# Four mixers and two feed-forwards in one kernel: 83 steps of two stage lists stand ahead of another one

## What is computed

```python
def layer0(h):
    h = sandwich(h, pre, post, even_mixer_2)      # stage "diff"
    return sandwich(h, pre, post, swiglu)         # stage "ffn0"
def layer1(h):
    h = sandwich(h, pre, post, odd_mixer_2)       # stage "ssm"
    return sandwich(h, pre, post, swiglu)         # stage "ffn1"
```

```python
def even_mixer_2(t):
    proj = t @ w_in
    y_a = diff_attention(proj[..., :1536])   # 4 heads: softmax(q1 k1) - lam * softmax(q2 k2), times v, rmsnorm
    y_b = conformer_conv(proj[..., 1536:])   # u * sigmoid(g), depthwise causal conv of 31 taps, layernorm, silu
    return concat([y_a, y_b]) @ w_out
def odd_mixer_2(t):
    proj = t @ w_in
    y_c = s5_ssm(proj[..., :256])            # complex diagonal state space, 16 groups of 64 states, gelu, gate
    y_d = mla_attention(proj[..., 256:])     # 6 heads, q and kv from low-rank latents, softmax, times v
    return concat([y_c, y_d]) @ w_out
```

## Time and profile before

| | |
|---|---|
| time before, median of 3 runs | 1879.53 us (1877.82 to 1880.75) |
| the profiled execution's own time | 1878.99 us |
| its span, first to last instruction | 1877.2 us |
| busy: TensorE, VectorE, ScalarE, GpSimd | 1744.0, 934.0, 763.7, 938.5 us |
| mean granted TensorE clock | 0.971 of full speed |
| stage `diff`, about 590 to 850 us | between two closings of other stages |
| stage `ssm`, about 1235 to 1485 us | |

### The profile page before, as it was taken

The page is one execution under the profiler, slowest core; times in us unless marked ns, Lnnn a source line. Parts: engine busy times, 40 slices in busy tenths (PEclk is TensorE's granted clock), DMA queues, the critical chain, the costliest instruction groups (busy, mean ns, idle before and its releaser), DMA issues.

```text
span 1877.2 us, 21115 instructions
## 1 busy us (share of the span) xinstructions
PE 1744.0 (93%) x7872; PEld 1345.4 (72%) x7872; DVE 934.0 (50%) x1490; ACT 763.7 (41%) x1306; POOL 938.5 (50%) x1108
## 2 busy tenths in 40 slices
PE   9999989999989989789999999998879899999997
PEld 6766558677767766468888888875445788888886
DVE  2043345766837799527723313366547573042344
ACT  4264555465465324645332223352333553222232
POOL 5433124457944553025555656569124456465563
PEclk9999999999999999799999999999879999999999
DMA  5211112222102211013233233211001123323231
GB/s 206 90 60 64 34 40 94 68 68 79 52 28 90 78 68 57 0 57 102 90 102 101 90 101 100 92 57 56 12 12 34 57 90 101 102 90 101 90 101 68
DMA packets 39702, 139.96 MB, mean 75 GB/s; under 512 B 4528, under 2 KB 4656, under 8 KB 39472
## 3 DMA queue, kind: packets, MB, share of 16 engines
q1 hardware_dynamic: 39600, 138.61, 22.0%
HBM read 136.50 MB, written 2.10 MB: 74 GB/s over the span
## 4 chain that ended last, share of the span: by engine, by line
PE 75%; DVE 13%; ACT 6%; POOL 3%; issue 3%; DMA 0%; SPq 0%; DVEq 0%; ACTq 0%; POOLq 0%
PE ps L713 17%; PE ps L715 16%; PE ps L714 16%; DVE ps L2060 3%; PE ps L784 1%; PE ps L786 1%; PE ps L785 1%; POOL wl L2987 1%; PE ps L1458 1%; PE ps L812 1%; DVE ps L925 1%; PE ps L1002 1%; PE ps L1000 1%; PE ps L1001 1%; PE ps L734 1%
## 5 line engine op out<-in xcount | busy, mean ns | idle before, releaser
L2987 POOL TENSOR_TENSOR wl<-raw,wh 128x256 fp32r<-128x256 f32 x988 | 802.7, 844 | 819.5 <-ACT wh L858 807.8
L858 ACT ACTIVATE wh<-raw 128x1024 fp32r<-128x1024 f32 x246 | 259.5, 1056 | 502.2 <-PE ps L715 448.0
L713 PE MATMUL ps<-hh,wh 128*128 128x512 f32 x1052 | 432.9, 412 | 18.4 <-DVE arena L2023 4.7
L715 PE MATMUL ps<-hh,wl 128*128 128x512 f32 x1052 | 412.5, 392 | 0.0
L714 PE MATMUL ps<-hl,wh 128*128 128x512 f32 x1052 | 412.3, 392 | 0.0
L713 PEld LDWEIGHTS ps<-hh,wh 128*128 128x128 f32 x1052 | 199.3, 189 | 78.0 <-issue 14.8
L713 PE MATMUL ps<-mh,wh 128*128 128x512 f32 x540 | 223.4, 414 | 23.7 <-DVE ml L2088 4.0
L714 PEld LDWEIGHTS ps<-hl,wh 128*128 128x128 f32 x1052 | 199.6, 190 | 46.0 <-issue 7.2
L715 PEld LDWEIGHTS ps<-hh,wl 128*128 128x128 f32 x1052 | 198.9, 189 | 42.7
L715 PE MATMUL ps<-mh,wl 128*128 128x512 f32 x540 | 212.5, 393 | 0.0
L714 PE MATMUL ps<-ml,wh 128*128 128x512 f32 x540 | 212.3, 393 | 0.0
(11 more groups left out here) (491 smaller groups left out, 2715.4 us busy)
## 6 DMA issues: line engine op xcount, KB each, us to landing
raw<-in_w SPq DMA_DIRECT2D x246, 512.0 KB, 3.3
x<-in_x SPq DMA_DIRECT2D x8, 256.0 KB, 6.7
out<-x SPq DMA_DIRECT2D x8, 256.0 KB, 2.0
arena<-in_rope SPq DMA_DIRECT2D x3, 512.0 KB, 4.2
arena<-in_dec SPq DMA_DIRECT2D x1, 1024.0 KB, 7.1
mats<-in_mats SPq DMA_DIRECT2D x1, 576.0 KB, 7.7
raw<-in_w SPq DMA_DIRECT2D x2, 256.0 KB, 3.9
arena<-in_lw SPq DMA_DIRECT2D x1, 512.0 KB, 4.1
```

The source lines that it names most:

```text
L713: e.matmul(ps[b][:], a, xh, start=first, stop=False)
L715: e.matmul(ps[b][:], l, xh, start=False, stop=final).then_inc(pe.sem, pe.up(*step))
L858: e.activation(wh[:, n % NHL, :], raw[:, n % NRAW, :], ACT.Copy).then_inc(rounded.sem, rounded.up(n))
L2987: e.tensor_tensor(wl[:, n % NHL, cut(i, 2)], raw[:, n % NRAW, cut(i, 2)], wh[:, n % NHL, cut(i, 2)].bitcast(F32), SUB).then_inc(split.sem, ...
```

## The change

A table `AHEAD` gives for `diff` 45 and for `ssm` 38 pairs (step, other). `settled` goes through them in order and calls `ahead` for each, so a step goes right before the other one, forward or back in the list (a later pair may move what an earlier one placed). `even` and `odd` have no entries. No step is added or dropped, and none of kind `w`, `t` or `vw` is a moved one. The pairs that the text below speaks of:

```diff
+AHEAD = {
+    "diff": [
...
+        (('r3', 4), ('r1', 5)), (('e', ('dq', 0)), ('cv', 2, 10)), (('fn', 1, 1), ('r2', 8)), (('fn', 0, 2),
+        ('fn', 1, 3)), (('cv', 0, 30), ('cv', 1, 2)), (('cv', 1, 30), ('cv', 2, 9)), (('v3', 2), ('pe', ('p',
+        5))), (('v3', 3), ('pe', ('p', 7))), (('e', ('dk', 3)), ('cv', 3, 26)), (('fn', 0, 0), ('fn', 1, 1)),
+        (('v3', 0), ('pe', ('p', 3))), (('cv', 1, 0), ('cv', 0, 23)), (('r3', 3), ('w', ('dq', 3), 1)),
+        (('cv', 1, 29), ('cv', 2, 2)), (('v3', 1), ('v2', 2)), (('cv', 3, 0), ('w', ('dk', 0), 7)), (('fn', 4,
...
+        1), 1)), (('e', ('ub', 1)), ('cv', 0, 6)), (('cv', 3, 2), ('r1', 0)), (('rb', ('dk', 1)), ('cv', 3,
...
+        ('fn', 4, 2)), (('v1', 2), ('w', ('p', 5), 2)), (('r4', 8), ('fn', 3, 1)), (('pe', ('p', 5)), ('w',
+        ('p', 5), 2)), (('v2', 0), ('v2', 1)), (('v2', 1), ('r3', 8)), (('cv', 3, 27), ('cv', 3, 28)), (('r2',
+        7), ('cv', 3, 24)), (('cv', 3, 26), ('cv', 3, 27)), (('r3', 6), ('cv', 3, 24))],
+    "ssm": [
+        (('ze', 0), ('w', ('zg', 0), 0)), (('s2', 5), ('s3', 4)), (('r4', 13), ('s1', 5)), (('z1', 0), ('r1',
+        14)), (('an', 2), ('ka', 0)), (('s1b', 7), ('r3', 23)), (('r4', 4), ('r3', 6)), (('r3', 21), ('pe',
...
+        0)), (('r2', 21), ('an', 7)), (('r1', 18), ('w', ('p', 1), 0)), (('r1', 12), ('s4', 2)), (('s4', 0),
+        ('r4', 3)), (('r4', 11), ('qa', 2)), (('z4', 0), ('s2b', 4)), (('e', ('un', 3)), ('r2', 2)), (('e',
+        ('kn', 5)), ('s1', 4)), (('r1', 10), ('s3', 3)), (('s2b', 4), ('s3', 4)), (('s2', 4), ('vw', 4)),
+        (('r2', 12), ('r4', 9)), (('s3b', 0), ('s3b', 1))],
+}
+
+def settled(stage, steps):
+
+    for step, of in AHEAD.get(stage, ()):
+        steps = ahead(steps, step, of)
+    return steps
+
+STEPS = {"even": settled("even", steps_even()), "odd": settled("odd", steps_odd()), "diff": settled("diff", steps_diff()), ...
```

More of the change, by code:

```diff
@@ L424, in steps_ssm @@
     return out + closing(4)
-STEPS = {"even": steps_even(), "odd": steps_odd(), "diff": steps_diff(), "ffn0": steps_ffn(first=[("ds", 0)], f1=[("ds", 1)], f2=[("ds", 2)], f3=[("ds", 3)], f5=[("ds", 4)], f7=[("ds", 5)],
+AHEAD = {
+    "diff": [
[14 rows of a table added]
+    "ssm": [
[11 rows of a table added]
+}
[3 more added lines that the diff above has]
+    return steps
+STEPS = {"even": settled("even", steps_even()), "odd": settled("odd", steps_odd()), "diff": settled("diff", steps_diff()), "ffn0": steps_ffn(first=[("ds", 0)], f1=[("ds", 1)], f2=[("ds", 2)], f3=[("ds", 3)], f5=[("ds", 4)], f7=[("ds", 5)],
                                                                          f8=[("ds", 6)], f9=[("ds", 7)]),
-         "ssm": steps_ssm(), "ffn1": steps_ffn(final=True)}
+         "ssm": settled("ssm", steps_ssm()), "ffn1": steps_ffn(final=True)}
 def weights(stage, g):
```

## The result

The changed kernel takes 1820.5 us as the median of its runs (1820.08 to 1821.95), the kernel before 1879.9 in the runs beside it: a ratio of 0.969, with a 95% interval from 0.9678 to 0.9702. That is 59 us where 38 were forecast. The sign was right.

A forecast was written before the change was run, and what follows sets the result against it. TensorE was taken as the engine to watch, VectorE as the convolution's bound. Terms of 14.5 (third mixer) and 27 us (fourth) sum to 41.5, less about 3.5: 38 gained, so 1841 us; range 1830 to 1851 (0.59), 8 in 10 1824 to 1863.

The forecast's parts named there:

- 3 for clock: Fourth mixer, 1352 to 1412: 3 us gained because the piece had lost 10 us of full-speed clock.
- 1352 to 1412: Fourth mixer: softmax steps moved ahead of steps they waited behind gain 12 us, from 4 to 18.
- 813 to 840: End of third mixer: spreading the v1 and v2 steps and moving v3 forward gains 8 us, from 5 to 10.
- 751 to 797: Third mixer: reordered ScalarE and softmax steps gain 3.5 us, from 0 to 7; most of 14 us idle stays.
- The rival for 0.12: Both mixers: with gaps closed, half of the 35 us of missing full-speed clock returns, so 1824 us; chance 0.12.
- 1276 to 1352: Fourth mixer: later an 2, earlier softmax rows and other moves gain 10 us, from 4 to 15.
- The discount: Whole kernel: about 3.5 us taken off the summed gain for hand-over waits that appear when one is gone.
- slower, by the clock: Both mixers: new gaps keep TensorE at the lower clock, matmuls cost 82 us more, so 1923 us; chance 0.04.
- 619 to 751: Third mixer's convolution, VectorE the bound: 0 us up to 684 (-1 to +1.5), then 3 us (0 to 5).
- the lighter VectorE: Fourth mixer, 1276 to 1352: later s3b 0 and an 5 shorten scans; with the softmax rows, 4.5 us.
- 1412 to 1476: End of fourth mixer: softmax steps, s1 6 and ze moved ahead gain 5 us, from 2 to 7.
- next input late: Both mixers: ScalarE or VectorE work replaces removed waits, so only about 22 us gained, 1857 us; chance 0.21.

The follow-up runs named there:

- third_only: Kernel before with only the 45 moves of the third mixer: 1861.1 us, ratio 0.9901.
- fourth_only: Kernel before with only the 38 moves of the fourth mixer: 1841.5 us, ratio 0.9795.
- piece_1352: Kernel before with only the 14 moves that act between 1352 and 1412 us: 1866.6 us, ratio 0.9924.
- without_piece_684: Changed kernel without the 17 moves that act between 684 and 751 us: 1821.7 us, ratio 0.9692.
- short_waits_before: Kernel before, order unchanged, with 25 extra unread matmuls in waits between 1352 and 1410 us, three of them in short waits: 1872.5 us, ratio 0.9966.

## Why the prediction was right and wrong

**What failed is the term for the clock.** The prediction said "3 for clock" in 1352 to 1412, and that half of the 35 us "returns" only by a rival, for 0.12. Measured: 21.6 us of matmul time between the same steps, seven times as much. In 813 to 840 the prediction saw the 3.0 us that the clock hides and counted little of it (its 8 is 7.1 of idle, less 1, plus 1.9); outside these two pieces it counted none. Piece by piece it is largest where the clock was lowest among the pieces that TensorE sets: -8.0 and -5.9 us in the fourth mixer (0.89 to 1.00, 0.83 to 0.92), -3.6 at the end of the third (0.89 to 1.00). The argument against, "in 751 to 797 most of the idle stays", was right for that piece (9.3 of 14.0 us) and said nothing of the others, from which most of the idle time went: 6.7 of 15.8, 1.8 of 11.7 and 0.35 of 7.1 us are left. A rule of thumb, found afterwards, would have done better: where the idle time of a piece goes, take its missing clock as going with it. For the three pieces that gives 0.11 x 76, 0.17 x 60 and 0.11 x 27, together 21.5 us; they gave 17.5 (8.0, 5.9 and 3.6, so the second was far off). The rival for 0.12 had the mechanism and nearly the size, half of the 35 us or 17.5.

That long waits lower the clock in these pieces is shown by the fillers. How much of the 21.6 us is the change's is less certain. By whole mixers the matmul time fell by 7.9 and 15.4 us in the changed kernel, by 6.1 and 12.4 in third_only and fourth_only with the same orders: 23 against 18. Beside that the unmoved 619 us in front had 5.0 us *more* matmul time in the changed kernel's profile, and an unmoved 1276 to 1352 had 2.6 us more in piece_1352.

**The discount was too large.** I took 3.5 us off for "waits that appear when one is gone". They appear (3.17, 3.27, 2.36 us above), but inside the pieces and their terms; idle time fell by 37.1 against at most 37.6, so no more than 0.5 was due. The discount speaks of eight pieces joined; there are seven.

**One rival was priced wrongly.** The same matmuls at a clock lower by a ratio take longer by that ratio: "slower, by the clock" should read 278 x (0.95 / 0.78 - 1) + 235 x (0.93 / 0.78 - 1) = 61 + 45 = 106 us and not 82. Nothing hung on it; both clocks rose.

**By piece.** *619 to 751*: 0 and 3 forecast, 2.0 measured. `cv 3 30`, the last tap, ends 133.0 us behind the opening's last `sq` before and after (617.87 to 750.87; 620.17 to 753.19), which the prediction named as the sign that 684 to 751 "gave nothing". VectorE is the bound, as said. The move of `e dq 0` took away its 1.54 us, but the next bank that TensorE needs is emptied by `e ub 3`, whose place in VectorE's line the move doesn't touch; the prediction priced the wait that it named and not this next one. The 2.0 us come at the end. `v1 0` and `ln 0` of the changed kernel on TensorE:

```profile
751.00 2.42 PE L2013 MATMUL ps<-arena 128*128 128x512 f32 x8 [0.35 <-ACT arena L2207]
753.26 3.60 PE L2033 MATMUL ps<-arena,mats 128*128 128x512 f32 x8
```

`ln 0` follows the end of `cv 3 30` (753.19) by 0.07 us. In the kernel before, TensorE was still in `v1 0` when the convolution ended (750.87), and `ln 0` began at 752.93, 2.06 us behind.

*751 to 797*: 3.5 forecast, 6.9 in the profile, 4.7 alone. The reason given, ScalarE nearly full, is right and is now the bound of 771 to 785 (13.51 of 13.70 us busy).

*813 to 840*: 7.1 us of idle forecast to go, 6.8 went, and the 1 us taken off for `v3 0` and `v3 3` never came; 3.6 us of matmul time came back besides. This reading of four steps in one bank was the best of the prediction.

*1276 to 1352*: 10 forecast, 17.0 measured, of which 9.1 idle. `an 2` gave about what was reckoned. But "the lighter VectorE" was wrong as it stood: VectorE is busy 50.13 us in this piece after and 48.31 before, `an 5` runs beside it (1292.46 to 1300.83) and not beside an idle VectorE, and the sixteen scans of the stage, 12.1 + 11.5 us before and 11.8 + 10.3 after, take 11.9 + 10.2 without the move of `s3b 0`. What `s3b 0` gives is its place behind the softmax maxima, and its own two instructions at half the length. The Trainium skill, page "SBUF — State Buffer", section "SBUF: two separate sides", still fits the single scan (2.29 us beside `an 5`); my estimate of 6 by it was no better than the 10, since neither counted the clock and both looked at the wrong VectorE instructions.

*1352 to 1412*: the waits of 3.41 and 5.57 us are both gone, idle -10.0 where 9 were counted without the clock.

*1412 to 1476*: 5 forecast, 5.0 of idle and 1.6 of clock measured.

The rival "next input late" (22 us) did not come true outside 684 to 797: the longest wait left in the fourth mixer is the 1.86 us before `r1 4`, where waits of 3.22, 3.37, 3.41 and 5.57 stood.

## What to carry to other kernels

Split a forecast into idle time and matmul time, and give the second its own term from the windows: a piece that loses its waits also loses most of its low clock, and here that was over a third of the gain. Give that second term the wider range: with one order fixed the idle time came out the same to 0.1 us, the matmul time of a mixer differed by up to 3. Do this only for pieces that TensorE sets; where ScalarE is full, a higher clock was worth nothing. When a wait for a read-out is taken away, look for the next product and who empties its bank, and when VectorE is the bound of a piece, measure the distance between its first and last step before believing in any gain there.

## What the runs showed of the hardware

Matmuls whose result nobody reads, put into long waits, made an unchanged order faster by 4 to 10 us. The clock behind a wait is also not fixed by its length: the same 2.56 us before `dq 0` were followed by matmuls of 0.39 us in the changed kernel and of 0.63 in without_piece_684. And long waits are not all: in the changed kernel the clock stands at its lower level when `v1 2` runs (4.29 us, where short_waits_before has 2.42), although the waits just ahead are of 0.35 to 0.46 us and TensorE is busy 42.41 of 44.20 us in that piece. Filling the three waits left the clock at 0.92. What the clock follows there stays open.

A GpSimd instruction beside a VectorE one made it longer: the two of `s3b 0` took 1.40 and 1.53 us beside `an 4` and 0.68 each with GpSimd idle.
